# Query and key slabs of the dilated attention as products with 512 moving columns, and earlier high parts

## The reference

```
def odd_mixer(xn, w_in, w_o, cos_f, sin_f):
    hcat = (xn @ w_in).reshape(b, s, DIL_GROUPS, 3, DIL_HEADS, HEAD_DIM)   # 3 groups, 16 heads of 64
    q = apply_rope(hcat[:, :, :, 0], cos_f, sin_f)
    k = apply_rope(hcat[:, :, :, 1], cos_f, sin_f)
    v = hcat[:, :, :, 2]
    return dilated_attention(q, k, v) @ w_o
...
        h = rms_norm_2(x, ffn_norm_gain[l])
        g = causal_dwconv(h @ w_ffn_gate[l], ffn_conv_w[l], ffn_conv_b[l])
        x = x + (jax.nn.gelu(g) * (h @ w_ffn_up[l])) @ w_ffn_down[l]
    return rms_norm_2(x, final_norm_gain)
```

## Time and profile before

| | |
|---|---|
| median of 3 runs | 1228.7 us (1226.69 to 1229.13) |
| the profiled execution's own time | 1229.48 us |
| its span, first to last instruction | 1227.7 us |
| TensorE matmuls busy | 1212.1 us, 99% |
| VectorE busy | 833.2 us, 68% |
| ScalarE busy | 642.9 us, 52% |
| GpSimd busy | 208.7 us, 17% |
| moved by DMA | 214.22 MB, 174 GB/s |
| granted TensorE clock, mean | 0.996 of full |

### The profile page before, as it was taken

One profiled execution on the slowest core, in us unless ns is written; L12 is line 12 of the kernel. 1 busy time (PEld: TensorE's weight loads), 2 busy tenths in 40 slices (PEclk: granted clock), 3 DMA queues, 4 the chain that ended last, 5 costly groups with the idle time before them and its releaser, 6 DMA issues.

```text
span 1227.7 us, 19290 instructions
## 1 busy us (share of the span) xinstructions
PE 1212.1 (99%) x7873; PEld 1076.9 (88%) x7873; DVE 833.2 (68%) x1171; ACT 642.9 (52%) x857; POOL 208.7 (17%) x160
## 2 busy tenths in 40 slices
PE   9999999999999999999999999999999999999898
PEld 9988998888899989999998888898878899888786
DVE  6878678755475666767879854487865566767753
ACT  5574465534445454445556544456576555555542
POOL 2500010000011201110310000010010785454100
PEclk9999999999999999999999999999999999999999
DMA  9723456555576555554355555554544455555541
GB/s 249 246 93 114 138 183 194 184 194 191 186 232 197 184 178 179 182 173 146 104 172 180 198 190 187 197 178 157 187 155 149 161 189 181 195 173 194 184 145 61
DMA packets 162070, 214.22 MB, mean 174 GB/s; under 512 B 5259, under 2 KB 117198, under 8 KB 161982
## 3 DMA queue, kind: packets, MB, share of 16 engines
q1 hardware_dynamic: 156574, 205.11, 50.7%
q10 hardware_dynamic: 5216, 7.42, 2.1%
q0 software_dynamic: 192, 0.46, 0.2%
HBM read 205.63 MB, written 1.05 MB: 168 GB/s over the span
## 4 chain that ended last, share of the span: by engine, by line
PE 78%; DVE 10%; ACT 5%; issue 3%; DMA 2%; SPq 0%; POOL 0%; ACTq 0%; DVEq 0%
PE ps L538 49%; PE ps L553 9%; PE ps L558 5%; PE ps L638 4%; ACT whi L1148 3%; DVE wlo L1602 3%; PE ps L735 3%; PE ps L772 2%; PE ps L743 2%; PE ps L580 2%; DVE TA L2255 1%; DMA raw<-in_ev_w_in_dram 1%; DMA TB<-TA 1%; DVE TB L2263 1%; DVE TA L2249 1%
## 5 line engine op out<-in xcount | busy, mean ns | idle before, releaser
L1602 DVE TENSOR_TENSOR wlo<-raw,whi 128x2048 fp32r<-128x2048 f32 (+1 forms) x167 | 387.0, 2320 | 192.7 <-ACT whi L1148 192.5
L1148 ACT ACTIVATE whi<-raw 128x2048 fp32r<-128x2048 f32 x188 | 357.5, 1905 | 154.5 <-PE ps L538 134.7
L553 PE MATMUL ps<-XHL,whi 128*128 128x512 f32 x800 | 198.8, 393 | 0.0
L553 PEld LDWEIGHTS ps<-XHL,whi 128*128 128x128 f32 x800 | 144.5, 189 | 26.4
L538 PE MATMUL ps<-XHL,whi 128*128 128x256 f32 x848 | 152.9, 285 | 0.0
L538 PE MATMUL ps<-whi,HH 128*128 128x512 f32 x384 | 148.3, 393 | 3.2 <-ACT whi L1148 3.2
L538 PE MATMUL ps<-whi,HL 128*128 128x512 f32 (+1 forms) x416 | 149.6, 375 | 0.0
L538 PE MATMUL ps<-whi,XHL 128*128 128x512 f32 (+1 forms) x576 | 145.3, 345 | 0.0
L538 PE MATMUL ps<-wlo,HH 128*128 128x512 f32 x368 | 144.1, 392 | 1.1 <-DVE wlo L1602 1.1
L2342 POOL TENSOR_TENSOR wlo<-raw,whi 128x512 fp32r<-128x512 f32 x88 | 119.4, 1388 | 142.1 <-ACT whi L1148 141.8
L538 PEld LDWEIGHTS ps<-XHL,whi 128*128 128x128 f32 x848 | 130.5, 191 | 0.6 <-issue 0.4
(11 more groups left out here) (271 smaller groups left out, 1788.6 us busy)
## 6 DMA issues: line engine op xcount, KB each, us to landing
raw<-in_mlp_w_dram SPq DMA_DIRECT2D x64, 1024.0 KB, 5.3
raw<-in_od_w_in_dram SPq DMA_DIRECT2D x36, 1024.0 KB, 5.2
raw<-in_w_in_dram SPq DMA_DIRECT2D x24, 1024.0 KB, 5.1
raw<-in_w_ffn_gate_dram SPq DMA_DIRECT2D x12, 1024.0 KB, 5.2
raw<-in_w_ffn_up_dram SPq DMA_DIRECT2D x12, 1024.0 KB, 5.2
raw<-in_w_ffn_down_dram SPq DMA_DIRECT2D x12, 1024.0 KB, 5.0
TB<-TA ACTq DMA_DIRECT2D x96, 64.0 KB, 3.7
raw<-in_w_branch_dram SPq DMA_DIRECT2D x6, 1024.0 KB, 5.0
```

The source lines that it names most:

```text
L553: pe.matmul(b[m][:, :], w[m][c][0], XHL[:, c, :], start=c == 0, stop=False)
L1148: act.activation(whi_of(n), raw_of(n), ACT.Copy, scale=1.0).then_inc(*tell(s_whi, ("whi", n)))
L1602: dve.tensor_tensor(wlo_of(n), raw_of(n), f32(whi_of(n)), ALU.subtract).then_inc(*tell(s_wlo, ("wlo", n)))
```

## The change

- The "qk" slabs from i = 2 on are made by `beside` instead of `features` or `features_low_last` (weights' low parts last for i below 6).
- For these ScalarE makes the two copies of `copies` instead of one, VectorE adds with `added` into `TA` and multiplies by the cosines from there. "copied" is now VectorE's event.
- The four transfers of a swap are issued by SyncE for all 24, on the queue of the loads, just ahead of the load of slab n + 5, and wait for "copied".
- ScalarE: in the early slabs `ahead` comes before the copy; beside attention the first slab's `ahead` comes before the unit's exponentials; in the last mlp `ahead(FD)` comes before the last gelu.
- VectorE: `ahead(FD)` comes behind the last convolution, before the low part of step 10 and z of step 11.
- TensorE: the first four FD slabs of the first half take the low weights last.

The diff, cut to its core:

```diff
# TensorE
                 elif kind == "qk":
                     if i > 1:
-                        (features_low_last if i < 6 else features)(n, x)
+                        beside(n, x, late=i < 6)
...
-                        product(b[t][:, :], ht, w_ready(n, 4, 0, 512), event, first=k == 0, last=k == 5)
+                        product(b[t][:, :], ht, w_ready(n, 4, 0, 512), event, first=k == 0, last=k == 5,
+                                late="right" if q == 0 and k < 4 else False)
# ScalarE
-            def odd_slab(i):
+            def odd_slab(i, begun=False):
                 n, (kind, hb, g, half) = SLAB_ODD + i, DILATED[i]
-                if i == 0 or i >= EARLY:
+                if i == 0 or i >= EARLY and not begun:
                     ahead(n)
...
                 k = swaps[0] % 2
-                b = take(("slab", n), [("rotated", swaps[0] - 2)] if swaps[0] > 1 else ())
-                act.activation(TA[k][:, :], b[:, :], ACT.Copy, scale=1.0).then_inc(*tell(s_act_out, ("copied", n)))
                 if 0 < i < EARLY - 1:
                     ahead(n + 1)
-                once.wait_ge(*at(("copied", n)))
-                for p in range(4):
-                    q = p ^ 1
-                    act.dma_start(TB[k][32 * p:32 * p + 32, :], TA[k][32 * q:32 * q + 32, :]).then_inc(
-                        *tell(s_swap[k], *([("swapped", swaps[0])] if p == 3 else []), by=16))
+                if i < 2:
+                    b = take(("slab", n))
+                    act.activation(TA[k][:, :], b[:, :], ACT.Copy, scale=1.0).then_inc(*tell(s_act_out, ("copied", n)))
+                else:
+                    copies(n, TA[k], ("rotated", swaps[0] - 2))
                 swaps[0] += 1
...
             for s in range(35):
+                beside = BESIDE[s] if s < len(BESIDE) else ()
+                for i in beside[:1]:
+                    ahead(SLAB_ODD + i)
                 attend(ODD, 32, s)
-                for i in BESIDE[s] if s < len(BESIDE) else ():
-                    odd_slab(i)
+                for i in beside:
+                    odd_slab(i, begun=i == beside[0])
...
+                if j == 11:
+                    ahead(FD)
                 once.wait_ge(*at(("ffn conv", j)))
...
-            for k in range(6):
+            for k in range(1, 6):
                 ahead(FD + k)
# VectorE
-                b = take(("slab", n), [("copied", n)])
-                dve.tensor_tensor(pair(QKV[hb % 3][3 * g + w]), pair(b[:, :]), twice(RP[:, 0:S]), ALU.mult).then_inc(
-                    *tell(s_dve_out, ("taken", "slab", n)))
+                to = pair(QKV[hb % 3][3 * g + w])
+                if i < 2:
+                    b = take(("slab", n), [("copied", n)])
+                    dve.tensor_tensor(to, pair(b[:, :]), twice(RP[:, 0:S]), ALU.mult).then_inc(
+                        *tell(s_dve_out, ("taken", "slab", n), ("scaled", n)))
+                else:
+                    v = TA[rotated[0] % 2]
+                    added(n, v, v, ("copied", n))
+                    dve.tensor_tensor(to, pair(v[:, :]), twice(RP[:, 0:S]), ALU.mult).then_inc(*tell(s_dve, ("scaled", n)))
...
-                if j < 11:
-                    ahead(FF + 2 * j + 1)
+                ahead(FF + 2 * j + 1 if j < 11 else FD)
                 if j:
                     ffn_low(j - 1)
...
-            for k in range(6):
+            for k in range(1, 6):
                 ahead(FD + k)
# SyncE
+            def swap(k):
+
+                once.wait_ge(*at(("copied", turned_slabs[k])))
+                for p in range(4):
+                    q = p ^ 1
+                    sp.dma_start(TB[k % 2][32 * p:32 * p + 32, :], TA[k % 2][32 * q:32 * q + 32, :]).then_inc(
+                        *tell(s_swap[k % 2], *([("swapped", k)] if p == 3 else []), by=16))
+
             for n in range(7, SLABS):
+                if n - RAW in turned_slabs:
+                    swap(turned_slabs.index(n - RAW))
                 load(n)
```

More of the change, by code:

```diff
@@ L420, in ahead_of @@
             return [1, 2] if n == 0 else [n + 2] if n + 2 < SLABS else []
+        turned_slabs = [SLAB_ODD + i for i, (kind, *_) in enumerate(DILATED) if kind == "qk"]
         pieces = {s: [(k, j) for k in range(3) for j in range(4)][max(0, s - 22) if s > 23 else 0:s - 21] for s in range(23, 34)}
@@ L1722, in attend, with added @@
                     outputs(group_of(first + s - 3))
-            def added(n, to, copy):
+            def added(n, to, copy, *events):
                 for m in range(2):
@@ L1728, in added @@
                     v = slice(m * S, m * S + S)
-                    dve.tensor_tensor(to[:, v], b[:, 0:S], copy[:, v], ALU.add).then_inc(*tell(s_dve_out, ("taken", "beside", n, m)))
+                    dve.tensor_tensor(to[:, v], b[:, 0:S], copy[:, v], ALU.add).then_inc(*tell(s_dve_out, ("taken", "beside", n, m), *(events if m else ())))
                 once.wait_ge(*at(("taken", "beside", n, 1)))
@@ L1974, in rotate @@
                     once.wait_ge(*at(("sine", k)))
-                    once.wait_ge(*at(("taken", "slab", SLAB_ODD + DILATED.index(("qk", hb, g, w)))))
+                    once.wait_ge(*at(("scaled", turned_slabs[k])))
                     dve.tensor_tensor(dst, dst, TB[k % 2][:, :], ALU.add).then_inc(*tell(s_dve, ("odd", hb, g, w), ("rotated", k)))
```

## The result

The changed kernel takes **1218.4 us** (1218.19 to 1218.81), the kernel before beside it 1228.9. The ratio is 0.9912 with a 95% interval of 0.9898 to 0.9926: 9.1 to 12.5 us faster, where 12.0 were forecast. Its profiled execution took 1218.49 us with a span of 1216.6, 11.1 us less than the span before.

The account below looks back on a forecast made before the run. TensorE, busy 99% of the span, was taken to bound the kernel. Gains of 6.8 + 3.8 + 1.4 = 12.0 us took the profiled 1229.5 to 1217.5, less 0.8 for the median: 1216.7 us, range 1214.0 to 1221.8.

Parts of the forecast that it names:

- Part 1: Last product: making the third slab's high part before the last gelu removes its wait and slow stretch; gain 6.8 us.
- the 3.3 us for whi: Last product, third slab: share of the 7.1 us loss that TensorE spends waiting for the high part.
- The half clock: Last product: rest of the 7.1 us loss, TensorE at 1.2 instead of 2.4 GHz behind its 3.2 us wait.
- the wait for wlo: Last product, third slab: 1.5 us of the 7.1 us loss, TensorE waiting for the low part.
- FD + 3: Last product's fourth slab: late next, wait 0.2 to 0.3 us; as rival 1.5 to 2.5 us, 1218.5 to 1221, chance 0.12.
- Part 2: 22 of 24 query and key slabs: 512 moving columns mean 16 fewer matmuls each; 0.175 us a slab, 3.8 us.
- The rival with 2.5 ns a matmul: Query and key slabs: widening saves only 0.04 us each, 0.9 instead of 3.8 us, 1219.6 us; chance 0.04.
- Part 3: Beside attention, 17 slabs: extra VectorE and ScalarE work costs nothing; pairs 14.28 us, VectorE 84% busy; bounds +3 and -1 us.
- the ring: Beside attention: high part, low part, multiply, rotation, maxima, exponentials, next high part; lap 7.4 to 8.0 us, opened by the move.
- the rival had 8.3: Beside attention: ring stays closed, lap 8.3 against 7.31 us, 1236.6 us; chance 0.06 together with late loads.
- VectorE keeps the old pace: Beside attention: steps stay at 7.31 us through VectorE's in-order waits, costing 3.0 us, 1219.7; chance 0.13.
- Part 4: Swaps on the loads' queue: nobody waits beside attention; early slabs lose 1.4 of 1.7 us of low-part waits; bounds +1, -1.7.

Follow-up runs that it names:

- the order alone: Kernel before, with only the low weights taken last for four slabs of the last product; high part as late as before: 1225.2 us, ratio 0.9973.
- the dilated edits alone: Changed kernel with the edits in the last mlp and last product undone: 1225.5 us against 1228.3 for the kernel before, ratio 0.9977.
- without the order: Kernel before with the last product's third slab's parts made early, but low weights not taken last: 1221.4 us, ratio 0.9943.
- narrow: Changed kernel with all query and key slabs made as before, 48 matmuls of 256 columns, one copy, no adds: 1219.8 us, ratio 0.9931.
- wide: Changed kernel with the loads of slabs 5 and 6 of the dilated part issued ahead of swaps 0 and 1: 1217.3 us, ratio 0.9907.
- the ring left closed: Changed kernel, but beside attention the high part is made behind the exponentials again: 1228.9 us, ratio to the kernel before 0.9996.

## Why the prediction was right, and where it was off

**Part 1** was right in place and size: forecast 6.8 us, 6.9 between the profiles and 7.2 by itself. Of its three terms, the 3.3 us for whi held, and the order alone took the wait for wlo down to 0.2 us. The half clock, the remaining 2.3 us, was there in the profiles of before and of the dilated edits alone, and absent in that of the order alone behind the same wait. So "it fell behind a stretch in which TensorE stood still" is right as to where it falls, and too strong as a rule that it must. For the kernel before, the mean granted clocks show it in nearly every execution, so that counting it in full was right; one profile alone could not have told that. The next thing late was FD + 3, as forecast; only without the order does its wait show (1.1 us).

**Part 2**, a size off by a little: 0.16 us a slab and 3.5 in all (14.32 against 14.63 for a pair), forecast 0.175 and 3.8. I had divided the best pieces of the mlps; the first piece of a slab behind attention takes 1.87 instead of 1.84. The two kernels without a wait at slab 6, narrow and wide, are 3.7 us apart. The rival with 2.5 ns a matmul (0.9 us) is refuted by the pairs.

**Part 3** was right, and the experiment on it is the most telling: with the ring left closed the wide form costs 5.6 us in the dilated stretch instead of gaining, and eats up most of part 1's gain with it. Its lap was 8.16 us where the rival had 8.3; the price of 17 us, for which the rival let all 17 slabs pay, came out at some 10. The lap of before, "7.4 to 8.0 us", was read from the longer of two alternating steps: the high part behind the one at 499.86 started 6.94 us later, and over the stretch pairs kept to TensorE's 14.63. VectorE's share came out at 80% (forecast 84%), wlo stopped waiting for whi, and the exponentials' wait for the maxima shrank to 1.0 us and less. The rival "VectorE keeps the old pace" was wrong.

**Part 4** was the step that failed. "So 1.4 of the 1.7 us go" did not come about: 1.2 us stayed in the profile after, 1.6 in the second one. I had let the load of slab 5 land 5.1 us after its issue, at 355; it was issued at 350.14 and ready at 356.48, 6.3 us later, and everything behind it (whi 5, copies, adds, wlo 5, wlo 6) was 1 to 1.5 us later than in my chain. Two loads and two swaps are issued between 347.1 and 353.9 there; that they slowed one another is likely (from 340 to 400 a load's median from issue to landing is 6.0 us, 5.2 before), but no run separates it. The mechanism was named ("the loads take the rotation's place") and its margin of 0.2 us was too thin to call a gain. With the two loads issued first the wait all but goes, and with the narrow form it goes too: the late load and the longer chain of copies and adds make it together. The second fault of the step was to read 1.7 us of waits in one execution as a fixed cost: for the same code they were 2.6, 0.3 and 0 in three others.

**The offset.** I took 0.8 us off, the difference between the median of before and its profiled run. After the change both agree (1218.39 and 1218.49), so this was scatter, and it is half of the 1.7 us by which the forecast missed; against the profiled run the forecast of 1217.5 is 1.0 low. Two sums of the prediction are off by less: 14.2 us from 1228.7 make 1214.5 for the lower end of the range, and 1216.7 and 20 make 1236.7, not 1236.6.

## What to carry to other kernels

When a step's work goes around two in-order engines (A makes x for B, B makes y for A, A makes the next x), compare one lap of that ring with the time of the bounding engine before work is added to it; an instruction that needs nothing from the ring belongs ahead of the one that does. A transfer that waits for a computing engine should not stand in front of loads that do not: issue the load first, unless the transfer is the urgent one. And a wait of a microsecond in one profile is worth counting only if it is seen in a second one.

## What the hardware showed

- A wait of 3.2 us of TensorE was followed by 6.8 us at half clock in two profiles (before, the dilated edits alone) and by none in a third (the order alone). The mean granted clock lay at 0.997 or below in 49 of 52 executions of the kernel before, and in none of nine of the changed one. A wait of 2.1 us (swaps on ScalarE) was followed by 3.4 us at half clock; waits of 1.1 and 1.6 us by none.
- A 128x512 matmul of this type, with its own weights, starts every 0.227 to 0.230 us and a 128x256 one every 0.120: 16 matmuls fewer for the same columns save 0.16 us.
- SyncE issued a quarter of a swap in 0.59 us (median) and the load right behind in 0.58 us; a load alone took it 0.37.
